# Feeding TensorE's 256 moving columns in turns from two token blocks, four columns each, in a two-block transformer kernel

## The reference, cut to what matters

```python
z = einsum("bsd,dn->bsn", rmsnorm(x, g_mix), w_in)         # 1024 -> 4608
y_a, y_b = einsum(a, w_a_out), einsum(s, w_b_out)          # 512 -> 1024 each
x = x + einsum(g_a * y_a + g_b * y_b, w_o)                 # 1024 -> 1024
u = einsum(rmsnorm(x, g_ffn), w_up)                        # 1024 -> 5632
x = x + einsum(gelu(conv(u_gate)) * u_value, w_down)       # 2816 -> 1024
x = x + sigmoid(einsum(rmsnorm(x), w_ple_gate)) * einsum(p, w_ple)
x = rmsnorm(x, g_final)
proj = einsum(rms_norm(x), w_in_2)                         # 1024 -> 2304, then two attentions
x = x + rms_norm(einsum(mix, w_out_2))                     # 1024 -> 1024
f = einsum(gelu(g) * val, w_down_2)                        # g, val: conv of 1024 -> 8192; 4096 -> 1024
x = x + rms_norm(f)
```

## Time and profile before

| | us |
|---|---|
| median of 3 runs | 752.45 |
| the profiled execution | 752.84 |
| its span | 750.8 |
| PE busy, share of the span | 743.0, 99% |
| PEld busy | 722.7, 96% |
| DVE busy | 578.7, 77% |
| ACT busy | 452.0, 60% |
| POOL busy | 210.6, 28% |

### The profile page before, as it was taken

The page is one execution under the profiler, slowest core; times in us unless marked ns, Lnnn a source line. Parts: engine busy times, 40 slices in busy tenths (PEclk is TensorE's granted clock), DMA queues, the critical chain, the costliest instruction groups (busy, mean ns, idle before and its releaser), DMA issues.

```text
span 750.8 us, 16764 instructions
## 1 busy us (share of the span) xinstructions
PE 743.0 (99%) x5950; PEld 722.7 (96%) x5950; DVE 578.7 (77%) x1049; ACT 452.0 (60%) x765; POOL 210.6 (28%) x136
## 2 busy tenths in 40 slices
PE   9999999999999999999999999999999999999997
PEld 9999999999999999999999999999999999988885
DVE  6899986877887887434987794799999999973333
ACT  7645456556665665445765798876766666643431
POOL 0477642460000000343464003322112212212220
PEclk9999999999999999999999999999999999999999
DMA  8566553565555567544444344365555555666551
GB/s 307 182 217 205 184 166 127 197 201 195 194 180 189 190 204 250 198 162 152 159 161 139 115 134 125 111 199 200 192 190 195 180 184 196 210 212 193 186 179 56
DMA packets 37917, 135.48 MB, mean 180 GB/s; under 512 B 4464, under 2 KB 4720, under 8 KB 37872
## 3 DMA queue, kind: packets, MB, share of 16 engines
q1 hardware_dynamic: 37728, 134.86, 54.4%
q10 hardware_dynamic: 144, 0.00, 0.0%
HBM read 133.80 MB, written 1.05 MB: 180 GB/s over the span
## 4 chain that ended last, share of the span: by engine, by line
PE 89%; DVE 3%; ACT 3%; issue 2%; POOL 1%; DMA 1%; SPq 0%; DVEq 0%; POOLq 0%; ACTq 0%
PE bank L1901 25%; PE bank L1902 25%; PE bank L1903 25%; PE bank L2349 4%; PE bank L2348 4%; PE bank L2347 4%; DVE w_lo L1223 1%; ACT w_hi L787 1%; DMA raw<-in_w_in 1%; POOL X L755 1%; PE bank L2176 1%; ACT score L1079 0%; PE bank L2200 0%; PE bank L1959 0%; DVE sumsq L1813 0%
## 5 line engine op out<-in xcount | busy, mean ns | idle before, releaser
L1901 PE MATMUL bank<-h_hi,w_hi 128*128 128x256 f32 x1372 | 385.9, 281 | 0.3 <-DVE w_lo L1223 0.2
L1902 PE MATMUL bank<-h_lo,w_hi 128*128 128x256 f32 x1372 | 382.9, 279 | 0.0
L1903 PE MATMUL bank<-h_hi,w_lo 128*128 128x256 f32 x1372 | 382.8, 279 | 0.0
L787 ACT ACTIVATE w_hi<-raw 128x1024 fp32r<-128x1024 f32 (+2 forms) x243 | 258.9, 1068 | 93.2 <-PE bank L1903 41.3
L1223 DVE TENSOR_TENSOR w_lo<-raw,w_hi 128x1024 fp32r<-128x1024 f32 (+2 forms) x187 | 236.6, 1268 | 85.9 <-ACT w_hi L787 84.0
L1901 PEld LDWEIGHTS bank<-h_hi,w_hi 128*128 128x128 f32 x1372 | 257.9, 188 | 1.8 <-DVE w_lo L1223 0.7
L1902 PEld LDWEIGHTS bank<-h_lo,w_hi 128*128 128x128 f32 x1372 | 258.0, 188 | 0.0
L1903 PEld LDWEIGHTS bank<-h_hi,w_lo 128*128 128x128 f32 x1372 | 257.9, 188 | 0.0
L636 POOL TENSOR_TENSOR w_lo<-raw,w_hi 128x1024 fp32r<-128x1024 f32 (+1 forms) x56 | 139.0, 2485 | 382.9 <-ACT w_hi L787 374.7
L1281 DVE TENSOR_TENSOR bank<-bank,scales 128x256 f32<-128x256 f32 x116 | 49.5, 430 | 26.3 <-PE bank L1903 17.6
L1572 DVE SCALAR_TENSOR_TENSOR cg<-bank,vec,cg 128x255 f32<-128x255 f32 x108 | 51.5, 476 | 0.7 <-ACT cg L1019 0.6
(11 more groups left out here) (235 smaller groups left out, 963.2 us busy)
## 6 DMA issues: line engine op xcount, KB each, us to landing
raw<-in_w_up SPq DMA_DIRECT2D x108, 512.0 KB, 3.3
raw<-in_w_in SPq DMA_DIRECT2D x53, 512.0 KB, 3.4
raw<-in_w_down SPq DMA_DIRECT2D x32, 512.0 KB, 4.2
raw<-in_w_down SPq DMA_DIRECT2D x16, 704.0 KB, 4.2
raw<-in_w_o SPq DMA_DIRECT2D x8, 512.0 KB, 4.3
raw<-in_w_gate SPq DMA_DIRECT2D x8, 512.0 KB, 3.4
raw<-in_w_out SPq DMA_DIRECT2D x8, 512.0 KB, 3.3
raw<-in_w_b_out SPq DMA_DIRECT2D x4, 512.0 KB, 3.6
```

The costliest lines, as they stand in the source:

```text
L787: nc.scalar.activation(hi_of(u)[:, cols], raw[s][:, cols], ACT.Copy).then_inc(hi_ready, 1)
L1901: nc.tensor.matmul(ps, wh, hi[:, k, :], start=start and n == 0, stop=False)
L1902: nc.tensor.matmul(ps, wh, lo[:, k, :], start=False, stop=False)
L1903: last = nc.tensor.matmul(ps, wl, hi[:, k, :], start=False, stop=stop and n == len(ks) - 1)
```

## The change

Every operand of 256 columns in the three functions, the moving one and the bank that takes the result, is viewed as 32 x 2 x 4: four columns of the tokens 0 to 127, four of the tokens 128 to 255, the next four of the first block, and so on. The result column of each token stays in its place. The number of matmuls, their order, their weights, all waits and all work of the other engines stay. `down2` with its 512 columns and the attention's products are not touched. The number of instruction rows in the programs' order is the same on all engines, and on VectorE and ScalarE their orders are identical.

```diff
+            def in_turns(columns):
+
+                return columns.rearrange("p (b i e) -> p i b e", b=2, e=4)
+
             def products(ps, s, block0, ks, hi, lo, start, stop, ready=None, w=None):
 
+                ps = in_turns(ps)
                 w_of = w or (w_hi[s], w_lo[s])
                 for n, k in enumerate(ks):
...
-                    nc.tensor.matmul(ps, wh, hi[:, k, :], start=start and n == 0, stop=False)
-                    nc.tensor.matmul(ps, wh, lo[:, k, :], start=False, stop=False)
-                    last = nc.tensor.matmul(ps, wl, hi[:, k, :], start=False,
+                    x_hi, x_lo = in_turns(hi[:, k, :]), in_turns(lo[:, k, :])
+                    nc.tensor.matmul(ps, wh, x_hi, start=start and n == 0, stop=False)
+                    nc.tensor.matmul(ps, wh, x_lo, start=False, stop=False)
+                    last = nc.tensor.matmul(ps, wl, x_hi, start=False,
                                             stop=stop and n == len(ks) - 1)
...
@@ in lagging
-                            nc.tensor.matmul(ps, wh, hi[:, k, :], start=start and k == ks[0], stop=False)
-                            nc.tensor.matmul(ps, wl, hi[:, k, :], start=False, stop=False)
+                            x_hi = in_turns(hi[:, k, :])
+                            nc.tensor.matmul(in_turns(ps), wh, x_hi, start=start and k == ks[0], stop=False)
+                            nc.tensor.matmul(in_turns(ps), wl, x_hi, start=False, stop=False)
...
@@ in rounded_first
-                ps = in_tile(u)
+                ps = in_turns(in_tile(u))
```

More of the change, by code:

```diff
@@ L1919, in lagging @@
                         for ps, s in tiles:
-                            last = nc.tensor.matmul(ps, w_hi[s][:, behind * P:(behind + 1) * P],
-                                                    lo[:, behind, :], start=False,
+                            last = nc.tensor.matmul(in_turns(ps), w_hi[s][:, behind * P:(behind + 1) * P],
+                                                    in_turns(lo[:, behind, :]), start=False,
                                                     stop=stop and k is None)
@@ L2012, in rounded_first @@
             def rounded_first(u):
-                ps = in_tile(u)
+                ps = in_turns(in_tile(u))
                 for k in range(DC):
                     wh = w_hi[slot(u)][:, k * P:(k + 1) * P]
-                    nc.tensor.matmul(ps, wh, h2_hi[:, k, :], start=k == 0, stop=False)
-                    nc.tensor.matmul(ps, wh, h2_lo[:, k, :], start=False, stop=False)
+                    nc.tensor.matmul(ps, wh, in_turns(h2_hi[:, k, :]), start=k == 0, stop=False)
+                    nc.tensor.matmul(ps, wh, in_turns(h2_lo[:, k, :]), start=False, stop=False)
                 unit_here(u)
                 for k in range(DC):
-                    last = nc.tensor.matmul(ps, w_lo[slot(u)][:, k * P:(k + 1) * P], h2_hi[:, k, :],
-                                            start=False, stop=k == DC - 1)
+                    last = nc.tensor.matmul(ps, w_lo[slot(u)][:, k * P:(k + 1) * P],
+                                            in_turns(h2_hi[:, k, :]), start=False, stop=k == DC - 1)
                 last.then_inc(unit_done, 1)
```

## The result

The changed kernel takes 801.83 us (median of 4 runs, 801.69 to 802.5) against 752.42 us (752.36 to 752.64): a ratio of 1.0658, 95% interval 1.0639 to 1.0676. The forecast was 734 us, the range 720 to 800.

A forecast was written before the change was run, and what follows sets the result against it. The prediction took matmul count times spacing as the bound: 4.7 ns less for each of 5232 matmuls, limited by stage, summed 3.0+2.2+8.1+0+1.5+4.0 = 18.8 us, so 734 us from 752.84. The range was 720 to 800.

The forecast's parts named there:

- What bounds the kernel: In the three changed functions, time is a number of matmuls times a spacing: 5232 at 0.1167 us, 611 us.
- The excess of 10 ns as two streams in each other's way: At each 256-column matmul, 0.1167 against 0.1067 us: reads of weights and moving columns were said to interfere now and then.
- the price of the unseen form: For 5232 matmuls with operands in 16-byte runs, a spacing of 0.112 us was taken, 4.7 ns less than now.
- the transposes: Run of f32 transposes, 8 records of 128 columns, read as two passes each: 0.110 us, taken as nearest low-conflict row.
- The good end: Best spacing expected for the changed matmuls, 0.110 us, which would save 26.3 us and give 726.5 us.
- The idea of a gain from another way of reading: Reading moving columns from two blocks alternately would keep their distance from the weights' reads, saving 4.7 ns a matmul.
- slower, more conflicts: From `in` to `up2`, weights and moving columns stay side by side and collide: 770 to 805 us; chance 0.22.
- The rival of the result's columns: PSUM takes short runs at half rate, so each of 5232 matmuls needs 0.2133 us: 1259 us; chance 0.08.
- No change: Excess sits at the hand-over between loads, or each 16-byte line hit twice is free: stays at 752.8 us; chance 0.22.
- The caps by stage: Limits on each stage's gain from VectorE, ScalarE and their chains, such as at most 5.3 us in `in`.
- The cap in `up2`: VectorE's idle time, 2.5%, was to limit the stage's 7.2 us to 4.4; 4.0 was taken.
- the forecast of nothing: In `gate`, no gain: a chain over ScalarE and VectorE repeats every 2.97 us, while a unit's 24 matmuls take 2.80.

The follow-up runs named there:

- the groups: Lines of 32 equal matmuls each, added behind the last product of the kernel before, spacing read from the timeline; reads in turns of four took 0.1266 us.
- the first groups: Forty lines of 32 equal matmuls added behind the last product of the kernel before; plain control 0.1167 us, reads in turns of four 0.1266 us a matmul.
- the kernel with singles in turns: The kernel before with only the moving reads changed, to single columns from the two blocks alternately, results written plain: 731.2 us, ratio 0.9709.

## Why the prediction was wrong

- *What bounds the kernel* was right: a number of matmuls times a spacing. 5232 x 10 ns gives the loss within 3 us, and PE is without a gap in 200 us of `o`, `up` and `down` as before.
- *The excess of 10 ns as two streams in each other's way* was half right. A plain stream's spacing does hang on the weights' place (0.1141 to 0.1197 in the groups). But some of the excess is the moving stream's own: 512 plain columns with the weights from one column still take 0.2319 us against 0.2156 in singles. The inference that it belongs to the load, from the equal excess of 256 and 512 columns, rested on one pair of places. With the weights at 64 the groups agree with it (0.1197 and 0.2269 us, 13 and 14 ns too much), with the weights at 32 they don't (0.1167 and 0.2350, 10 and 22).
- *The failed step is the price of the unseen form.* "I take 0.112, ... nearest to the transposes: the pace is theirs, but every 16-byte run now jumps, which should leave a part of the excess." The pace was taken as what counts and the jump as an afterthought. The reverse is so: the spacing became 0.1267 us, and with the weights from one column, turns of four still cost 7 to 10 ns more than plain. The good end was bounded by a row with no jump in it; no row showed a jump, and a row that shares one property with the new form is no nearest row for the other. Nor did that row show the pace. That the transposes take two passes of 128 columns stands in no row: eight transposes left eight records, while the f32 matmul behind them left two each. 128 plain fp32r columns with their load take the same 3.52/32 = 0.1100 us (L2420 of the first groups, 0.1115 for its last 27 starts), so 0.110 is what a matmul with its load costs with 128 columns too, and says nothing of 256.
- *The idea of a gain from another way of reading* was not empty. Each line read twice, 128 columns for 256, takes 0.1116 us, and so do singles in turns. There the moving stream keeps up, and what is left is probably the load of weights, since half the columns, settled, take no less (0.1115).
- *The rival "slower, more conflicts"* had the size, an excess of 20 ns and 805 us, but not the mechanism: it laid it on weights and moving columns side by side, and with the blocks 128 columns apart the weights' place changes nothing in the groups' turns of four, and 2 ns at the side tiles. The range ended at 800, below the end at 805 that the text itself had worked out; cutting there left the result out.
- *The rival of the result's columns* is refuted: 753.4 us with only these changed. *No change*, by the rule of the two hits on a line, is refuted as well.
- *The caps by stage*, drawn up for a gain, can be held against the kernel with singles in turns, which had one. The stretches below hold the same matmuls in each kernel, to within two; all are us:

| stage | before | the change | singles in turns | gain forecast |
|---|---|---|---|---|
| `in` | 88.0 | 95.3 | 84.8 | 3.0 |
| end of `in`, `b_out`, `ple`, `a_out` | 60.0 | 64.1 | 59.4 | 2.2 |
| `o`, `up`, `down` | 200.0 | 216.9 | 191.8 | 8.1 |
| `gate` | 26.0 | 27.4 | 25.8 | 0 |
| `in2`, `out2` | 91.0 | 95.5 | 89.1 | 1.5 |
| `up2` | 180.0 | 194.6 | 172.8 | 4.0 |

The cap in `up2` was mis-sized. It was to be 4.4 us, VectorE's idle time, and the stage gained 7.2: in its 172.8 us VectorE is busy for 170.6, by its row

```profile
462.90:635.70 172.80, 172.21 (x1538) 171.74 (x1538) 170.61 (x308) 124.15 (x204) 41.77 (x23) 1.00 0.58 188
```

so it was 3 us quicker with nearly the same instructions and hardly held TensorE. Of 5232 x 5.0 = 26.2 us the kernel gained 21.8; what fell short did so mostly in `b_out` to `a_out`, `gate` and the attention's stages. In `gate` the forecast of nothing was nearly right, but 2.97 us is the period of ScalarE's and VectorE's chain: TensorE's own 24 starts took 2.80 us there too (365.17 to 367.97), with a wait only now and then.

What stays open: why singles in turns from two blocks run at full pace, while pairs in turns take 0.1644 to 0.1734 us and singles from four blocks 0.1431. That the reader keeps two lines at hand would fit the singles but not the pairs; it was not settled. A single price for every jump fits neither: singles jump most often and cost least. Nor is it known what sets a plain stream's steady state.

## What to carry to other kernels

A matmul stream that never waits still has a price per matmul that its operands' access pattern sets: compare the spacing of starts with the columns' time at the granted clock before looking for waits. When a change brings a pattern that no row shows, put a few dozen groups of it behind the kernel and read their spacing, then prove it in the whole kernel, since a spacing read in a group can be another steady state than the kernel's. In fp32r, matmuls whose moving columns alternate singly between two halves follow one another 4% faster here than plain ones (0.1116 against 0.1167 us), and storing the operand with even and odd tokens apart makes that usable.

## What was not expected of the hardware

- Reads of the moving operand: runs of 4, 8, 16 and 64 columns in turns from two blocks take 0.1266, 0.1231, 0.1200 and 0.1169 us for 256 columns, pairs 0.1644 to 0.1734, a step of two columns 0.2263, singles in turns 0.1116.
- Writes of the result in turns of four columns cost nothing in the whole kernel (753.37 against 753.07 us), and in pairs, in a group, nothing either (3.74/32 = 0.1169, L2405).
- The same plain operands ran at 0.1141 or at 0.1178 us, with nothing changed but the groups that had run before.
- In turns of four from blocks 128 columns apart the weights' place changes nothing (4.04 to 4.06 us for 32); from blocks 160 apart it does (0.1206 and 0.1263 us).
